# Two attentions between blocks: head work laid between weight blocks in the first, and the gate rows turned in two parts in the second

## What is computed

```python
def diff_attention(h, w_qkv, lam, subln_g, w_o, cos, sin, layer_idx):   # between FFN 2 and FFN 3
    q, k, v = jnp.split(h @ w_qkv, 3, axis=-1)          # 1024 x 3072
    # 8 heads; q and k of a head are two halves of 64, v is 128 wide; the first 16 of each 64 get a rotary turn
    def block(qb):
        sc = jnp.einsum('bqhcd,bkhcd->bhcqk', qb, k)
        p = jax.nn.softmax(sc, axis=-1)
        a = p[:, :, 0] - lam_full * p[:, :, 1]
        return jnp.einsum('bhqk,bkhe->bqhe', a, v)
    o = rms_norm(o, subln_g) * (1 - lam_init)           # per head
    return o.reshape(b, s, d) @ w_o                     # 1024 x 1024

# between FFN 3 and FFN 4, in second_block:
z = u @ w_in                                            # 1024 x 5640
ya = moba_attention(qa, ka, va)                         # 8 heads of 64, causal
hb = mlstm_chunkwise(qb, kb_, vb, i_pre, f_pre)         # 4 heads of 128, decays from two gate rows a head
yb = sigmoid(ob) * rms_norm(hb)
h = h + (sigmoid(ga) * (ya @ w_proj_a) + sigmoid(gb) * (yb @ w_proj_b)) @ w_out
```

## Time and profile before

| | us |
|---|---|
| median of 3 runs (1578.92 to 1581.75) | 1581.15 |
| the profiled execution | 1576.95 |
| its span in the trace | 1575.0 |
| PE busy | 1417.4 (90%) |
| DVE busy | 930.5 (59%) |
| ACT busy | 630.2 (40%) |
| POOL busy | 159.1 (10%) |

### The profile page before, as it was taken

How to read it: one execution, slowest core, us unless ns; L and a number is a source line. 1 busy time by engine, 2 the same in 40 slices (tenths; PEclk the granted TensorE clock), 3 DMA queues, 4 the chain that set the end, 5 groups by cost and what they waited for, 6 DMA issues and landing times.

```text
span 1575.0 us, 18098 instructions
## 1 busy us (share of the span) xinstructions
PE 1417.4 (90%) x6455; PEld 1141.5 (72%) x6455; DVE 930.5 (59%) x1056; ACT 630.2 (40%) x816; POOL 159.1 (10%) x196
## 2 busy tenths in 40 slices
PE   5589998799999999999965799999897799999997
PEld 2478886568887788887754588887685577788886
DVE  3367885747787577786344456454657343654452
ACT  2334433333433543335325453443454445443441
POOL 2000011110001200001030010001206000000000
PEclk9699999899999999999987799999998899999999
DMA  9677876448886688873440066455435323455450
GB/s 345 220 267 266 279 258 210 162 168 290 289 296 217 210 283 304 303 261 109 159 160 1 12 228 233 168 174 182 144 109 186 113 108 107 134 202 182 163 187 27
DMA packets 179764, 303.75 MB, mean 193 GB/s; under 512 B 8500, under 2 KB 122564, under 8 KB 179576
## 3 DMA queue, kind: packets, MB, share of 16 engines
q1 hardware_dynamic: 159272, 224.62, 42.0%
q0 software_dynamic: 20432, 78.32, 13.6%
HBM read 301.86 MB, written 1.05 MB: 192 GB/s over the span
## 4 chain that ended last, share of the span: by engine, by line
PE 37%; DVE 8%; ACT 4%; issue 2%; POOL 1%; DMA 1%; SPq 0%; POOLq 0%; ACTq 0%; DVEq 0%
PE ps L473 11%; PE ps L475 10%; PE ps L474 10%; DVE wlo L1584 3%; ACT whi L1115 1%; ACT arena L1367 1%; PE ps L624 1%; PE ps L827 1%; DVE xn L2005 1%; PE ps L563 0%; PE ps L836 0%; PE ps L997 0%; DVE small L1936 0%; DVE arena L1625 0%; DVE arena L1947 0%
## 5 line engine op out<-in xcount | busy, mean ns | idle before, releaser
L1584 DVE TENSOR_TENSOR wlo<-raw,whi 128x2048 fp32r<-128x2048 f32 x212 | 483.7, 2316 | 92.4 <-ACT whi L1115 92.3
L473 PE MATMUL ps<-whi,nthi 128*128 128x512 f32 (+1 forms) x1264 | 511.1, 404 | 16.0 <-DVE arena L1910 8.7
L475 PE MATMUL ps<-whi,ntlo 128*128 128x512 f32 (+1 forms) x1264 | 499.1, 395 | 0.0
L474 PE MATMUL ps<-wlo,nthi 128*128 128x512 f32 (+1 forms) x1264 | 499.0, 395 | 0.0
L1115 ACT ACTIVATE whi<-raw 128x2048 fp32r<-128x2048 f32 x212 | 396.9, 1910 | 133.1 <-PE ps L475 51.4
L473 PEld LDWEIGHTS ps<-whi,nthi 128*128 128x128 f32 x1264 | 243.4, 193 | 66.6 <-DVE arena L1910 10.0
L475 PEld LDWEIGHTS ps<-whi,ntlo 128*128 128x128 f32 x1264 | 242.3, 192 | 52.0
L474 PEld LDWEIGHTS ps<-wlo,nthi 128*128 128x128 f32 x1264 | 243.5, 193 | 48.1 <-issue 0.8
L473 PE MATMUL ps<-whi,hthi 128*128 128x512 f32 x440 | 174.4, 396 | 3.4 <-DVE htlo L1665 3.4
L1625 DVE SCALAR_TENSOR_TENSOR arena<-arena,cact 128x512 f32<-128x512 f32 x221 | 169.2, 766 | 8.8
L475 PE MATMUL ps<-whi,htlo 128*128 128x512 f32 x440 | 171.5, 390 | 0.0
(11 more groups left out here) (253 smaller groups left out, 960.9 us busy)
## 6 DMA issues: line engine op xcount, KB each, us to landing
raw<-in_ffn_w_gu SPq DMA_DIRECT2D x176, 512.0 KB, 4.9
arena<-in_mod_w POOLq DMA_DIRECT2D x69, 1024.0 KB, 7.7
raw<-in_ffn_w_down SPq DMA_DIRECT2D x88, 512.0 KB, 5.9
raw<-in_w_in SPq DMA_DIRECT2D x44, 512.0 KB, 4.3
raw<-in_w_gate_up SPq DMA_DIRECT2D x44, 512.0 KB, 4.8
raw<-in_diff_w_qkv SPq DMA_DIRECT2D x24, 512.0 KB, 4.5
raw<-in_w_down SPq DMA_DIRECT2D x22, 512.0 KB, 5.6
raw<-in_diff_w_o SPq DMA_DIRECT2D x8, 512.0 KB, 4.3
```

Of the source, the lines that this page charges most:

```text
L473: pe.matmul(o, hi, wh, start=start, stop=False)
L474: pe.matmul(o, hi, wl, start=False, stop=False)
L475: return pe.matmul(o, lo, wh, start=False, stop=stop)
L1584: v.tensor_tensor(wlo[:, s * PIECE:(s + 1) * PIECE], raw[:, r * PIECE:(r + 1) * PIECE], hi, ALU.subtract).then_inc(w_lo, 1)
```

## The change

In the first mixer the order on every engine is written out anew. The columns are computed as q, k, v of heads 0 to 3, then q, k, v of heads 4 to 7; only the first two blocks go through A and B, the other four are groups that go to the sum banks. Heads 0 to 4 stand between the groups of the qkv matrix, heads 5 to 7 between halves of `wo`, whose pieces are now ordered by half of k: the half that needs heads 0 to 3 only is done early. The turned weights use bank T instead of M, the mixed result bank M instead of a sum bank. POOL's rotary turn comes in three parts, its norm scales head by head, DVE's norm too. The last half of `wo` follows heads 4 to 7. In the second mixer `turn_rows` is done in two parts, the first after `group(2, 0, 0)` on `rows_step`, the second after `group(3, 0, 1)` on `rows_done`; DVE's copy is in two parts as well; one of ACT's splits moves from the start of the mixer to its end, so that ACT is one piece less ahead between; the wait for `ob_scaled` moves from ahead of the first `turn_pair` to after the second `scores`.

```diff
+        qkv_cols = [0, 1024, 2048, 512, 1536, 2560]
+        qkv_pieces = pieces_of_matrix(d["diff_w_qkv"], qkv_cols)
+        wo_pieces = [(kn(d["diff_w_o"], k0, 4, c0, BLK), 4) for k0 in (0, 4) for c0 in (0, BLK)]
+        WEIGHTS_AT, ATT_T = (3, 5, 7, 8, 11, 13, 16, 17), 17
...
                 first = n.next("turned").at
                 first_blocks(first)
-                for _ in range(4):
-                    columns(KT, first)
-                pe.wait_ge(roped, 2)
-                pe.wait_ge(drained[A], n.seen(A))
-                pe.wait_ge(drained[B], n.seen(B))
+                w, wo = {}, {}
+                def group(b, h, t):
+                    if t == 0:
+                        w[h] = views()
+                    if h == 0 and b >= 2:
+                        pe.wait_ge(qkv_read[t], b - 1)
+                    mm = block_half(ps[:, 2 * t + (b + 1) % 2, :], t, h, w[h])
+                    if t:
+                        mm.then_inc(w_used, 1)
+                    elif h:
+                        mm.then_inc(qkv_full, 1)
...
+                    pe.wait_ge(roped, 2 if h < 4 else 6)
...
+                def out_half(c, k, t):
+                    if t == 0 or (c, k) not in wo:
+                        wo[c, k] = views()
+                    if k == 0 and c == 0:
+                        sums_free(t, s)
+                        pe.wait_ge(qkv_read[t], 4)
+                    pe.wait_ge(nt_lo, 4 * again + 2 * k + t + 1)
+                    o = ps[:, 2 * t + c, :]
+                    for q in range(4):
+                        kk = 4 * k + q
+                        mm = three(o, nth[:, kk, t * P:(t + 1) * P], ntl[:, kk, t * P:(t + 1) * P],
+                                   wo[c, k][0][:, q, :], wo[c, k][1][:, q, :], kk == 0, kk == KT - 1)
+                    if t:
+                        mm.then_inc(w_used, 1)
+                    return mm
...
+                group(0, 0, 0)
+                group(0, 0, 1)
+                group(0, 1, 0)
+                turn_qk(0)
+                group(0, 1, 1)
+                scores(0)
+                group(1, 0, 0)
+                turn_qk(1)
+                group(1, 0, 1)
+                scores(1)
+                turn_weights(0)
+                group(1, 1, 0)
+                mix(0)
+                turn_qk(2)
+                group(1, 1, 1)
+                scores(2)
+                turn_weights(1)
+                group(2, 0, 0)
+                mix(1)
+                turn_qk(3)
+                group(2, 0, 1)
+                scores(3)
+                turn_weights(2)
+                group(2, 1, 0)
+                mix(2)
+                group(2, 1, 1)
+                turn_weights(3)
+                group(3, 0, 0)
+                mix(3)
+                group(3, 0, 1)
+                turn_qk(4)
+                group(3, 1, 0)
+                scores(4)
+                group(3, 1, 1)
+                pe.wait_ge(heads_normed, 8)
+                again, s = n.next("turned").at, n.next("sums").at
+                for t in range(TB):
+                    for q in range(4):
+                        mm = pe.transpose(ps[:, 2 * t + 1, q * P:(q + 1) * P], qkv[:, t, q * P:(q + 1) * P], ident[:, :])
+                    mm.then_inc(early_turned, 1)
+                turn_qk(5)
+                scores(5)
+                turn_weights(4)
+                out_half(0, 0, 0)
+                mix(4)
+                turn_qk(6)
+                out_half(0, 0, 1)
+                scores(6)
+                turn_weights(5)
+                out_half(1, 0, 0)
+                mix(5)
+                turn_qk(7)
                 gate_rows()
-                pe.wait_ge(heads_normed, 2)
-                for t in range(TB):
-                    for h in range(2):
-                        turn_half(qkv, t, h)
-                whole_onto_sums(n.next("turned").at)
+                scores(7)
+                turn_weights(6)
+                out_half(1, 0, 1)
+                mix(6)
+                turn_weights(7)
+                mix(7)
+                pe.wait_ge(heads_normed, 16)
+                for t, b in enumerate((A, B)):
+                    turn_four(b, t, lambda t, q: qkv[:, t, (4 + q) * P:(5 + q) * P])
+                out_half(0, 1, 0)
+                out_half(1, 1, 0).then_inc(sums_done, 1)
+                out_half(0, 1, 1)
+                turn_join((0,))
+                out_half(1, 1, 1)
...
-                def turn_rows():
-                    pe.wait_ge(rows_done, 1)
+                def turn_rows(src):
                     o = bank(M)
-                    for g, src in enumerate((va_rows[3], va_rows[1])):
-                        for t in range(TB):
-                            mm = pe.transpose(o[:, (2 * g + t) * 4:(2 * g + t) * 4 + 4], src[:, t * P:(t + 1) * P],
-                                              ident[0:4, 0:4])
+                    for t in range(TB):
+                        mm = pe.transpose(o[:, 4 * t:4 * t + 4], src[:, t * P:(t + 1) * P], ident[0:4, 0:4])
                     mm.then_inc(filled[M], 1)
...
                 group(2, 0, 0)
+                pe.wait_ge(rows_step, 1)
+                turn_rows(va_rows[3])
                 group(2, 0, 1)
                 group(2, 1, 0)
                 group(2, 1, 1)
-                turn_rows()
                 group(3, 0, 0)
                 pe.wait_ge(conv_out, 8)
                 pe.wait_ge(pick_landed, 16)
                 decay_scores(0)
                 group(3, 0, 1)
+                pe.wait_ge(rows_done, 1)
+                turn_rows(va_rows[1])
                 group(3, 1, 0)
...
                     if h == 0:
-                        pe.wait_ge(ob_scaled, 1)
                         turn_pair(0)
                     scores(h)
+                    if h == 1:
+                        pe.wait_ge(ob_scaled, 1)
                     if h:
                         turn_probs(h - 1, n.seen(A) - 1)
...
+                blocks_head(j, (g_cols, shift), START["qkv"], keep)
+                act.wait_ge(lam_prod, 1)
+                nc.scalar.activation(lam[:, 2:4], lam[:, 0:2], ACT.Exp).then_inc(lam_exp, 1)
+                split(2)
+                block(0)
+                turned_qk(0)
+                split(1)
+                exps(0)
+                turned_qk(1)
+                split(1)
+                weights(0)
+                exps(1)
+                block(1)
+                mixed(0)
+                turned_qk(2)
+                split(1)
+                weights(1)
+                exps(2)
+                mixed(1)
+                turned_qk(3)
+                split(1)
+                weights(2)
+                exps(3)
+                block(2)
+                mixed(2)
+                split(1)
+                weights(3)
+                mixed(3)
+                split(1)
+                turned_qk(4)
+                block(3)
+                exps(4)
+                for t in range(TB):
+                    act.wait_ge(early_turned, t + 1)
+                    nc.scalar.activation(nth[:, 0:4, t * P:(t + 1) * P], ps[:, 2 * t + 1, :].rearrange("p (k s) -> p k s", k=4),
+                                         ACT.Copy).then_inc(nt_hi, 1)
+                turned_qk(5)
+                weights(4)
+                exps(5)
+                mixed(4)
+                turned_qk(6)
+                split(1)
+                weights(5)
+                exps(6)
+                mixed(5)
+                turned_qk(7)
                 gate_rows(1.0)
-                turned_hi()
-                split(2)
+                weights(6)
+                exps(7)
+                mixed(6)
+                split(1)
+                weights(7)
+                mixed(7)
+                turned_half_hi(0, 1, A)
+                turned_half_hi(1, 1, B)
...
                 n.next(M)
-                split(1)
                 pad(0, T)
...
                 turned_half_hi(1, 1, A)
+                split(1)
...
+                def normed_head(h):
+                    dve.wait_ge(heads_rstd, h + 1)
+                    for t in range(TB):
+                        o = qkv[:, t, h * P:(h + 1) * P]
+                        v.scalar_tensor_tensor(o, o, hss[:, 8 * t + h:8 * t + h + 1], subln, ALU.mult, ALU.mult)\
+                         .then_inc(heads_normed, 1)
+                split(1)
+                others(0)
+                tops(0)
+                split(1)
+                weigh(0)
+                tops(1)
+                split(1)
+                weigh(1)
+                others(1)
+                tops(2)
+                split(1)
+                weigh(2)
+                normed_head(0)
+                tops(3)
+                split(1)
+                weigh(3)
+                normed_head(1)
+                others(2)
+                split(1)
+                normed_head(2)
+                normed_head(3)
+                tops(4)
+                split(1)
+                others(3)
```

(81 more changed lines are left out.)

108 lines of the change are left out of this document (45 added, 63 removed).

## The result

The changed kernel takes 1522.8 us (median of 4 runs, 1521.69 to 1523.45) against 1580.37 us for the kernel before in the same session: a ratio of 0.9637, 95% interval 0.9623 to 0.9652, or 57.6 us less. Its profiled execution took 1523.37 us, with a span of 1521.6 us.

A forecast was written before the change was run, and what follows sets the result against it. PE sets the pace except in the two mixers, where it waits for other engines. Gains of 45 us in the first and 14 in the second, 59 in all, bring the median from 1581.15 to 1522 us, range 1507 to 1550.

The forecast's parts named there:

- The first mixer: The first mixer's stretch was to take 133.4 us in place of 179.0, a gain taken as 45 us.
- Each exposed piece: First mixer: waits of PE left uncovered, such as head 7's chain, `mix(7)` and `turn_join`, 12.4 us in all.
- the cover of the rotary turn: First mixer: POOL's rotary turns lie beside weight groups, behind block 1 with a group to spare, so cost nothing.
- The first rival: First mixer: the heads' chains don't fit and are late by 22.4 us, giving 1543 us; chance 0.22.
- The rule against the change: POOL contends with DVE's splits, 1.0 us more each; ten in the first mixer's heads are 10 us, counted as nothing.
- rows: Second mixer: `turn_rows` in two parts, with ACT one split less ahead, gains 5.5 us, between 3 and 9.
- one split less ahead: Second mixer: ACT no longer holds its first decay behind a split that waits for PE; within the 5.5 us for rows.
- `ob_scaled` and the split: Second mixer: earlier `turn_pair(0)` and `scores(0)`, ACT's split no longer waiting for PE: 5.5 us, between 2 and 8.
- The rest of the heads: Second mixer: 1.6 and 1.8 us of waits for ACT mostly go: 3 us, between 0 and 6.
- The second rival: Second mixer's edits do nothing: the wait only moves and 14 us shrink to 2, giving 1534 us; chance 0.12.
- The third: Rival, slower: first mixer's heads run step after step, 19.4 us a head, giving 1595 us; chance 0.03.
- The sum: Both mixers together: 45 + 14 = 59 us, bringing the median to 1522 us; chance 0.55.

## Where the prediction was right and where not

**The first mixer** was right in size and in all but two of its steps. Forecast were 133.4 us for the stretch, measured 132.2; a gain of 45, measured 44 to 45 between J1 and J2. PE's own work was put at 118 us and was busy 119.0. Each exposed piece stands in PE's timeline of the changed kernel:

```profile
849.76 0.66 PE L849 MATMUL ps<-ident,arena 128*128 128x128 f32 x4 [1.25 <-DVE arena L2082]
851.83 1.16 PE L860 MATMUL ps<-arena 128*128 128x128 f32 x8 [1.41 <-ACT arena L1457]
855.73 1.97 PE L782 MATMUL ps<-ident,arena 128*128 128x128 f32 x8 [2.74 <-DVE arena L2089]
858.35 0.77 PE L477 MATMUL ps<-whi,nthi 128*128 128x512 f32 x1 [0.65 <-DVE ntlo L1988]
872.14 2.05 PE L628 MATMUL ps<-rdiag,xres 128*128 128x128 f32 x16 [2.66 <-POOL rdiag L2483]
```

Head 7's chain 1.25 (forecast 1.1), `mix(7)` 1.41 (2.1), the norm 2.74 (2.9), the split of the last transposes 0.65 (0.9), `turn_join` 2.66 (2.9), with `scores(5)` 0.86 (1.0) and the gate rows 1.4 (1.5): 11.0 us where the sum had 12.4. One step that failed is the cover of the rotary turn, which was taken as hidden with a group to spare: it cost 2.3 us and some clock. I had followed the later parts of the turn and not the first, and had not let DVE's splits lengthen it. The other is the end of the stretch, where I had put 1 us for the first group of FFN 3:

```profile
885.34 2.05 PE L628 MATMUL ps<-rdiag,xres 128*128 128x128 f32 x16 [2.23 <-POOL rdiag L2483]
```

This is the second `turn_join`; it waits 2.2 us where it waited 0.2 before, and the first group of FFN 3 0.45. DVE starts its last addition of the join 3.0 us after PE's last product with `wo` (879.98 and 876.96 us) where it was 0.2 us (922.53 and 922.3): the work behind the first `turn_join` and a split are still ahead of it. That is why J1 to J2 fell by 43.9 us and the stretch by 46.8.

**The first rival** (chains late by 22.4 us in sum) did not come: seven of eight heads had margin, head 4 only 0.2 us. It was a matter of 2 us a head, though: with 2.3 us more in seven chains 7.2 us of wait appear, with 4.6 us more 21.7, nearly the rival's figure.

**The rule against the change** was weighed at the wrong place. In the heads nine splits took 2.30 us each, as without POOL, so its nothing in the sum was right. I had also misread. What ran beside the two splits of 6.65 us was the last instruction of the rotary turn and one long instruction for the diagonals, which takes 1.90 us where no split meets it. Kernel before, then the changed kernel, where the long one meets two of DVE's short steps (0.61 us for both elsewhere in the heads):

```profile
798.80 0.74 POOL L2334 TENSOR_TENSOR arena<-xn 128x256 f32<-128x256 f32 x1
799.65 3.80 POOL L2293 TENSOR_TENSOR xn<-ident,modc 128x1024 f32<-128x1024 f32 x1
```

```profile
815.44 1.90 POOL L2468 TENSOR_TENSOR xn<-ident,modc 128x1024 f32<-128x1024 f32 x1
815.51 2.25 DVE L2089 SCALAR_TENSOR_TENSOR arena<-arena,small 128x128 f32<-128x128 f32 x2 [2.87 <-POOL small L2497]
```

In the second mixer I let it cost nothing without a word, and there it decided: the wait at `decay_scores` was forecast as 6 us and was 8.8, the moved split had freed POOL to begin early. That is the term "rows": 5.5 us forecast, and from the end of (2, 1, 1) to the second `decay_scores` only 2.1 (23.6 to 21.5 us); alone, without the moved split, 4.5 to `scores(0)`. The sentence "one split less ahead" counted what ACT's split costs and not what it had held back.

**`ob_scaled` and the split** were forecast as 5.5 us, and gave 7.8 from the end of group (5, 0, 0) to the first product with v (29.4 to 21.6 us); `scores(0)` came 2.7 us earlier, as forecast (2.6). **The rest of the heads** was put at 3 us with a bound of 6, and was 6.0. Both were sized too low for one reason, the clock: behind J3 and up to J4 the waits fell by 7.6 us (25.0 to 17.4), the stretch by 15.0, and the clock over it rose from 0.91 to 0.95. The sum of the second mixer, 15 us in the profiles, is near the 14 forecast by luck: the errors had two signs. By the ratio of its edits alone it is 11 us (7 to 15). **The second rival** (wait of 10 us or more, nothing won) is excluded by the second mixer's edits on their own kernel, 0.9930 with an upper bound of 0.9956. **The third** (slower) is excluded by the result, and a head with its two groups takes 8.5 us on PE (789.16 to 797.67), where it would begin at 15.9 and I had 8.8.

**The sum** had 59 us; the medians have 57.6, the two profiled executions 53.6. Of the rest 3.0 us lie between J2 and J3 and 1.1 behind J4, where nothing was changed. The mechanism of the first mixer was right; that the median came within 1 us of the forecast is partly luck, with the second mixer's terms off in both directions and single profiles that differ by 3 us where the code is the same.

## What to carry to other kernels

Lay an idle chain between blocks of independent work only after writing down, head by head, how long the work between its two ends is: here those margins foretold the waits of a longer chain to within 1 us. When an edit lets an engine off the critical path start earlier, ask whom it now runs beside; here one wait on POOL was worth 7 us, as much as two of the change's own edits (the rows and the split together gave 6 by their ratio). A wait that is filled with a group saves only up to the next engine's chain, so look for that before moving work.

## What the runs showed of the hardware

The clock behind a wait isn't decided by that wait alone. The changed kernel and the same kernel once more, at the same place and behind the same wait:

```profile
1044.87 1.02 PE L567 MATMUL ps<-ident,arena 128*128 128x128 f32 x4 [2.27 <-DVE arena L1772]
```

```profile
1044.86 0.63 PE L567 MATMUL ps<-ident,arena 128*128 128x128 f32 x4 [2.27 <-DVE arena L1772]
```

In the first the 24 matmuls that follow are 0.325 us apart on the mean, in the second 0.23: 2 to 3 us from one wait of 2.27 us, once paid and once not. J2 to J3, the same code in all kernels, is therefore 203.0 to 207.8 us over the profiles. The windows of 8.73 and 11.88 us above are a second such pair, behind a wait of 1.8 us. A single profile can't settle an edit of 3 us. The waits of PE inside the two mixers, which repeat to within 0.1 us in the changed kernel's two profiles, show better what an edit moved, though not what it is worth; outside the mixers some sums of waits differ by up to 0.4 us (L628, 16.8 and 16.4).

The other finding is how POOL and DVE share: in the meetings looked at here, the instruction that started first kept its time, and the other was held until the first ended. A split that started first took 2.3 or 2.4 us and held POOL's 0.46 us to 2.4 or 2.5. POOL's 1.90 us instruction started 0.07 us ahead of two short steps of DVE, and these took 2.25 in place of 0.61 us. It is the order and not the length: at 798.80 us an instruction of POOL of 0.74 us started 0.15 us ahead of a split and kept its time, and the split took 2.75 us; POOL's long one then started inside that split and was held (3.80 us), and the next split in turn behind it (6.65 us for the two). Where POOL's instructions of 0.7 to 0.9 us alternate with DVE's short steps, these take 1.5 to 2.3 times as long on the mean (0.49 to 0.74, 0.35 to 0.81), and the splits among them 2.65 in place of 2.28 us.
